# Summed squares, block layouts, in-place y and a gated opening in an eight-core decoder trunk

## The chip, the cores and the metric

The program runs on one Trainium2 chip, on all 8 cores. Each core computes half of one prompt (2048 of 4096 tokens, with a halo of 144 positions ahead of them that it computes again) and 64 of the 512 sample rows. No core talks to another. The metric is device time in microseconds (us) of the slowest core.

## The reference

Layer 0 is an attention and convolution layer, layer 1 a pooling layer. Around each mixer stand two half-step SwiGLU feed-forward blocks, so there are four in all:

```python
def rmsnorm(x, g):
    y = x * lax.rsqrt(jnp.mean(x * x, axis=-1, keepdims=True) + 1e-6)
    return y * g

# per layer
x = x + 0.5 * swiglu(rmsnorm(x, g[0]), gate, up, down)      # 1024 -> 2816 -> 1024
h = rmsnorm(x, g[1])
x = x + mixer(h)   # layer 0: windowed attention | short convolution, projected out
                   # layer 1: causal means over 2, 4, 8, 16 rows minus h, grouped linear
x = x + 0.5 * swiglu(rmsnorm(x, g[2]), gate2, up2, down2)
# at the end
y = rmsnorm(x, final_gain)
```

The outputs are y for prompt and sample tokens and the updated key, value, convolution and pooling states.

## The kernel before

Features lie on the partitions (8 tiles of 128, index `k` or `m`), tokens on the free axis. The 2256 tokens of a core are done in two groups one after the other: group 0 has 1168 tokens (144 halo, 1024 prompt), group 1 has 1088 (1024 prompt, 64 sample). A group is cut into three subs: 400, 384 and 384 columns in group 0, 384, 384 and 320 in group 1. Later stages of group 0 need fewer halo columns, and the first sub shrinks to 272 and then to 256. The sample tokens are the last 64 columns of group 1.

One Python function, `emit`, lists all operations in program order. `Sched.op` puts a semaphore wait wherever an operation reads or overwrites what another engine or a transfer touches. Each engine then runs its own operations strictly in that listed order. So the order of the listing sets what an engine is stuck behind; no planner moves anything.

- **Weights** go through a ring of 17024 bf16 columns. `pump` (L312) issues a transfer from the POOL queue as soon as space is free. Eight gate-and-up tiles fit; they are converted from f32 by the transfer.
- **Norms.** `Norm.sq` squares row `k` of x on ACT into a bf16 buffer, and `Norm.flush` lets PE multiply it by a column of 1/1024 (`onesD`), one matmul for each block of at most 128 tokens. These "ones matmuls" accumulate the mean of squares over the 8 rows. `Norm.stat` takes the root on ACT and the reciprocal on DVE, `Norm.rb` broadcasts it with f32 matmuls, and `Norm.hs` makes the scaled input h (`sb_hT`) with 8 DVE instructions.
- **ffn** has a staged first part (gate and up products, `evac` with Silu on ACT and a product on DVE) and then `rows_out` for the down product. A down row is 22 matmuls for one of the 8 rows `m` and one sub. In its middle `half` flushes the squares of an earlier row. DVE adds the row to x (`add`, L380 into `sb_xs`) and ACT squares the new x. The last 2 or 4 rows are done sub by sub, so that the norm of one sub is made beside the next (`ms`). Two PSUM banks (`yb`) take turns as the row's output. The last sub's norm is made at the start of the next stage (`tail_hooks`).
- **The mixer** makes k, q and v of all columns of a sub (`rope_unit`, `v_unit`), and in `chb_unit` the three products of the convolution branch. These units fill the PE between steps of the attention.
- **The pooling stage** (`pool_stage`) makes window sums as matmuls with scaled identities (`p_stage`), copies them to `pp` on ACT, and multiplies by the group weights (`z_stage`). The sums of the sample tokens are made by `sample_pool` on POOL (L1229, L1247), from an h that DVE writes, into `spp`. One DVE copy (L372) then puts all of `spp` into `pp` ahead of the third sub.
- **Ends.** At the start SP's queue loads constants and then x of group 0 (one sub in four pieces, two subs whole), and POOL's queue loads eight weight tiles. At the end `out_ops` writes y into one of two staging buffers (`ystg`, `sb_reg` in the profile) and stores it with one transfer for each sub. The third sub uses the first one's buffer again.

## Time and profile before

| | |
|---|---|
| runs of the kernel before | 2514.12, 2624.45 and 2623.94 us; median 2623.94 us |
| profiled execution | 2516.68 us |
| its span on the slowest core | 2515.1 us |
| spans of the eight cores | 2507.5 to 2515.1 us |
| PE (matmul) busy | 2409.5 us, 96% |
| DVE busy | 816.8 us, 32% |
| ACT busy | 587.7 us, 23% |
| POOL busy | 288.6 us, 11% |
| PE's share of the chain that ended last | 91% |

PE is busy for all but 105.6 us of the span. A row of the timeline gives the start in us, the busy time in us, the engine, the source line, the operation, what it writes and reads, the shape and the count; in brackets stands the idle time ahead of it and what ended it. Matmuls overlap, so the distance between two starts tells more of their price than the busy time does.

### The profile page before, as it was taken

The numbers are of one execution on the slowest core, as the hardware profiler recorded it, in microseconds if no ns is written. First come the engines' busy times: TensorE is split into PE (matmuls) and PEld (weight loads), VectorE is DVE, ScalarE is ACT, GpSimd is POOL, SyncE is SP. The second block draws the span as 40 slices with busy tenths as digits, with TensorE's granted clock in tenths as the row PEclk, the third lists the DMA queues.
The fourth block names the chain that finished last, engine by engine and source line by source line (L and its number), as shares of the span: only waits on it lengthen the run. The fifth ranks groups of instructions, "written<-read, shape, count | busy, mean of one in ns | idle before, by whom it ended". The sixth has DMA issues, their size and how long they took to land.

```text
span 2515.1 us, 45298 instructions; the slowest of 8 cores (2507.5 to 2515.1 us)
## 1 busy us (share of the span) xinstructions
PE 2409.5 (96%) x16668; PEld 1544.1 (61%) x16668; DVE 816.8 (32%) x1705; ACT 587.7 (23%) x1420; POOL 288.6 (11%) x512
## 2 busy tenths in 40 slices
PE   4999999999999999999999999999999999979996
PEld 2555655666666666666666665566666666646664
DVE  2221287522132214321432128752213221342213
ACT  3111145211111113212231114421111111221111
POOL 0001133000000010001000014300000000020000
PEclk9999999999999999999999999999999999989998
DMA  9544323344445442444574453245453544415432
GB/s 199 109 66 70 56 38 52 63 77 75 70 67 84 69 75 34 68 71 76 111 159 67 73 73 58 45 68 77 70 73 57 84 68 64 67 31 78 67 60 72
DMA packets 72407, 184.99 MB, mean 74 GB/s; under 512 B 9376, under 2 KB 24032, under 8 KB 72160
## 3 DMA queue, kind: packets, MB, share of 16 engines
q0 software_dynamic: 53424, 157.18, 41.5%
q1 hardware_dynamic: 18768, 24.90, 3.8%
q8 instruction: 140, 2.29, 0.4%
q14 instruction: 75, 0.61, 0.1%
HBM read 329.25 MB, written 11.99 MB: 136 GB/s over the span
## 4 chain that ended last, share of the span: by engine, by line
PE 91%; DVE 3%; DMA 3%; issue 1%; POOL 1%; ACT 1%; DVEq 0%; SPq 0%; ACTq 0%; POOLq 0%
PE ps_gupair L359 68%; PE ps_bk L359 22%; DMA sb_xs<-xin 2%; DVE sb_hT L380 1%; PE ps_bk L363 1%; DMA y_main<-sb_reg 0%; POOL sb_reg L1229 0%; ACT sb_sqr L407 0%; DVE sb_xs L380 0%; DVE sb_reg L380 0%; DVE sb_ovl L375 0%; DVE sb_xs L375 0%; POOL sb_reg L984 0%; DVE sb_rp L375 0%; POOL sb_reg L1247 0%
## 5 line engine op out<-in xcount | busy, mean ns | idle before, releaser
L359 PE MATMUL ps_gupair<-sb_hT,sb_wring 128*128 128x384 bf16 (+4 forms) x8696 | 1339.3, 316 | 4.4 <-DVE sb_xs L380 1.7
L359 PEld LDWEIGHTS ps_gupair<-sb_hT,sb_wring 128*128 128x128 bf16 x8696 | 849.9, 98 | 482.6 <-issue 11.9
L375 DVE TENSOR_TENSOR sb_ovl<-sb_rp,ps_gupair 128x384 bf16<-128x384 f32 (+4 forms) x536 | 282.8, 528 | 960.3 <-PE ps_gupair L359 942.8
L407 ACT ACTIVATE sb_rp<-ps_gupair 128x384 f32<-128x384 f32 (+4 forms) x528 | 247.4, 470 | 999.0 <-PE ps_gupair L359 997.3
L359 PE MATMUL ps_bk<-sb_ovl,sb_wring 128*128 128x384 bf16 (+4 forms) x2304 | 382.4, 316 | 1.4 <-DVE sb_xs L375 1.3
L359 PE MATMUL ps_gupair<-sb_ovl,sb_wring 128*128 128x384 bf16 (+4 forms) x2304 | 382.0, 315 | 0.0
L407 ACT ACTIVATE sb_sqr<-sb_xs 128x384 bf16<-128x384 f32 (+4 forms) x336 | 163.0, 501 | 647.8 <-DVE sb_xs L380 481.2
L359 PEld LDWEIGHTS ps_bk<-sb_ovl,sb_wring 128*128 128x128 bf16 x2304 | 216.6, 98 | 116.4 <-issue 3.4
L359 PEld LDWEIGHTS ps_gupair<-sb_ovl,sb_wring 128*128 128x128 bf16 x2304 | 216.3, 98 | 112.4
L327 POOL DMA_DIRECT2D sb_wring<-wgu x176 | 93.3, 532 | 1270.1 <-PE ps_gupair L359 1046.2
L380 DVE SCALAR_TENSOR_TENSOR sb_hT<-sb_xs,sb_cst,ps_bk 128x384 bf16<-128x384 f32 (+4 forms) x280 | 145.1, 582 | 9.0 <-PE ps_bk L359 9.0
L359 PE MATMUL ps_bk<-sb_hT,sb_wring 128*128 128x384 bf16 (+3 forms) x808 | 141.2, 320 | 5.0 <-DVE sb_reg L413 3.4
L380 DVE SCALAR_TENSOR_TENSOR sb_xs<-ps_gupair,sb_xs 128x384 f32<-128x384 f32 (+4 forms) x96 | 51.1, 532 | 268.7 <-PE ps_gupair L359 258.5
L327 POOL DMA_DIRECT2D sb_wring<-wd x128 | 67.5, 528 | 593.9 <-PE ps_gupair L359 466.6
L380 DVE SCALAR_TENSOR_TENSOR sb_xs<-ps_bk,sb_xs 128x384 f32<-128x384 f32 (+4 forms) x96 | 51.1, 532 | 227.3 <-PE ps_bk L359 221.6
L359 PEld LDWEIGHTS ps_bk<-sb_onesD,sb_sqr 128*128 128x128 bf16 (+2 forms) x984 | 70.4, 97 | 81.0 <-issue 53.4
L359 PE MATMUL ps_bk<-sb_onesD,sb_sqr 128*128 128x1 bf16 (+2 forms) x984 | 73.8, 166 | 47.9 <-ACT sb_sqr L407 46.7
L359 PEld LDWEIGHTS ps_bk<-sb_hT,sb_wring 128*128 128x128 bf16 x808 | 73.0, 98 | 56.6 <-issue 19.0
L984 POOL TENSOR_SCALAR sb_reg<-sb_reg,sb_st 128x256 bf16<-128x256 f32 x68 | 68.3, 1013 | 101.2 <-DVE sb_st L976 89.1
L407 ACT ACTIVATE sb_reg<-ps_gupair,sb_st 128x256 f32<-128x256 f32 x136 | 62.0, 465 | 4.5 <-DVE sb_st L390 4.5
L359 PE MATMUL ps_gupair<-sb_hT,sb_Dg 128*128 128x384 bf16 (+1 forms) x360 | 57.3, 315 | 1.2 <-ACT sb_reg L370 1.2
L359 PE MATMUL ps_bk<-sb_cst,sb_rr 128*128 128x128 f32 (+2 forms) x246 | 40.7, 301 | 10.9 <-DVE sb_rr L482 8.6
(111 smaller groups left out, 791.7 us busy)
## 6 DMA issues: line engine op xcount, KB each, us to landing
sb_wring<-wgu POOLq DMA_DIRECT2D x176, 512.0 KB, 5.7
sb_wring<-wd POOLq DMA_DIRECT2D x128, 352.0 KB, 5.0
sb_wring<-wmi POOLq DMA_DIRECT2D x46, 256.0 KB, 5.4
y_main<-sb_reg SPq DMA_DIRECT2D x4, 1536.0 KB, 16.4
sb_xs<-xin SPq DMA_DIRECT2D x3, 1536.0 KB, 40.6
sb_wring<-wmo POOLq DMA_DIRECT2D x16, 256.0 KB, 5.1
...
```

What stands on the lines that cost most here:

```text
L327: OP("pool", lambda e, d=dst, s=src: e.dma_start(out=d, in_=s), [], [[("wring", off * 2, (off + n) * 2)]], dma=f"w{t % NWK}")
L359: OP("pe", lambda e: e.matmul(out.ap, lhsT=lhsT.ap, rhs=rhs.ap, start=start, stop=stop), [lhsT, rhs], [out])
L363: OP("pe", lambda e: e.transpose(out.ap, in_.ap, idn.ap), [in_, idn], [out])
L375: OP(eng, lambda e: e.tensor_tensor(out=out.ap, in0=a.ap, in1=b.ap, op=op), [a, b], [out])
L380: OP("dve", lambda e: e.scalar_tensor_tensor(out=out.ap, in0=a.ap, scalar=sc, in1=b.ap, op0=op0, op1=op1), rd, [out])
L407: OP("act", lambda e: e.activation(out=out.ap, in_=in_.ap, func=func, **kw), rd, wr)
L984: OP("pool", lambda e, o_=o_, i_=i_, sc_=sc_: e.tensor_scalar(out=o_.ap, in0=i_.ap, scalar1=sc_.ap, scalar2=None, op0=ALU.mult), [i_, sc_] ...
```

## The change

It has these parts.

1. `Norm.sqa` stands in for `Norm.sq` in the four down products of both groups (`presum=True`). ACT squares row 0 into `rp(s.idx)` and every other row into `rp(3)`, both f32; DVE adds the two after each row, and after the last row writes the sum as bf16. PE then does one set of ones matmuls for each sub where it did eight. The other norms (after the mixers and of the loaded x) keep `sq`.
2. x and y lie in blocks in DRAM: each sub of x, and each stored piece of y, is contiguous for each partition. The host arranges them.
3. y of group 1 is written over x (`Y = X(s, k)`), and two rows at a time are stored as soon as they are made. Group 1's last down product goes in 4 + 4 rows where it was 6 + 2.
4. In the opening, x of subs 1 and 2 comes in two halves each; the weight transfers from the third tile on wait for the last piece of x of sub 0; mask, convolution state, cache copies, cosines and sines wait until the third tile of the first product is there.
5. Queries are made for columns from 128 on, gate and h products of the convolution from 126 on, where both were made from 0 on in group 0.
6. The sample tokens' pooling goes ahead of the scaled h of the third sub, and ACT copies its result row by row.

```diff
@@ Norm @@
+                def sqa(self, k, s):
+                    c = slice(0, s.n)
+                    if k == 0:
+                        act(rp(s.idx, c), X(s, k), AF.Square)
+                        return
+                    act(rp(3, c), X(s, k), AF.Square)
+                    if k < KC - 1:
+                        tt(rp(s.idx, c), rp(s.idx, c), rp(3, c), ALU.add)
+                        return
+                    sl = cnt["sq"] % NSQ
...
+                    tt(sqr(sl, c), rp(s.idx, c), rp(3, c), ALU.add)
+                    self.pend.append((None, s, sl))
@@ rows_out @@
-                    nxt.sq(m, ns)
+                    if presum:
+                        nxt.sqa(m, ns)
+                    else:
+                        nxt.sq(m, ns)
@@ pump @@
-                    OP("pool", lambda e, d=dst, s=src: e.dma_start(out=d, in_=s), [],
+                    OP("pool", lambda e, d=dst, s=src: e.dma_start(out=d, in_=s), gate.get(t, []),
@@ mixer @@
+                csubs = g.subs(max(g.mix - 2, 0))
-                    return [k_unit(s)] + [q_unit(j, s) for j in range(4)] + [v_unit(s)]
+                    return [k_unit(s)] + [q_unit(j, msubs[s.idx]) for j in range(4)] + [v_unit(s)]
-                fill = qkv(subs[1]) + qkv(subs[2]) + [chb_unit(i, s) for i in range(4) for s in subs]
+                fill = qkv(subs[1]) + qkv(subs[2]) + [chb_unit(i, s) for i in range(4) for s in csubs]
@@ pool_stage @@
                             copy(pp(k, slice(0, np_)), pbk(slice(0, np_)), eng="act")
+                            if np_ < n:
+                                copy(pp(k, slice(np_, n)), spp(k), eng="act")
-                    if g.i == 1 and si == 2:
-                        c0 = g.S[0] - s.c0
-                        copy(pp(slice(0, KC), slice(c0, c0 + 64)), spp(), eng="dve")
                                 norm.rb(norm.subs[2])
+                                if g.i == 1:
+                                    q.q += sample_pool(g, subs[2], norm)
+                                    q.pop()
                                 q.q += norm.hs(norm.subs[2])
                                 if g.i == 1:
                                     q.q += outs(subs[2])
-                                    q.q += sample_pool(g, subs[2], norm)
@@ out_ops @@
+                if g.i == 0:
+                    yt = ystg[s.idx % 2]
+                    Y = lambda k: yt(k, slice(0, s.n))
...
+                else:
+                    Y = lambda k: X(s, k)
+                    src = xs[s.slot].ap
+                    d = s.base
...
+                for k in range(KC):
+                    out.append(lambda k=k: stt(Y(k), X(s, k), cs(C_GAIN + 6 * 8 + k), norm.r(s), ALU.mult, ALU.mult))
+                    if g.i == 1 and k % 2 == 1:
+                        out.append(lambda k=k: store(k - 1, k + 1))
@@ opening @@
             load_x(GROUPS[0], 0, 4)
-            load_x(GROUPS[0], 1)
-            load_x(GROUPS[0], 2)
+            s0 = GROUPS[0].subs(0)[0]
+            load_x(GROUPS[0], 1, 2)
+            load_x(GROUPS[0], 2, 2)
...
+            gate[2] = [X(s0, KC - 1)]
             pump()
-            dma("pool", maskb.ap, maskd[:, :, :], [], [maskb()], "msk")
...
+            def later():
+                rd = [aT(2, slice(0, 400))]
+                dma("pool", maskb.ap, maskd[:, :, :], rd, [maskb()], "msk")
...
@@ last ffn @@
-                    ms=(4, 4) if g.i == 0 else (6, 2))
+                    ms=(4, 4))
```

How this stands on the engines is shown at three places.

The first is POOL's queue at the start of the program, `sb_wring` being the weight ring. Before:

```order
L1420 UNCONDITIONAL_BRANCH [waits barrier_Pool_Activation_PE_DVE_SP_gather]
L327 DMA sb_wring<-wgu 128x2048 x8
L410 DMA sb_maskb<-maskd 128x1536
L327 DMA sb_wring<-wgu 128x2048 [waits s_pe,d_w0]
L327 DMA sb_wring<-wgu 128x2048 [waits s_pe,d_w1]
```

And now:

```order
L1474 UNCONDITIONAL_BRANCH [waits barrier_Pool_Activation_PE_DVE_SP_gather]
L328 DMA sb_wring<-wgu 128x2048 x2
L328 DMA sb_wring<-wgu 128x2048 [waits d_x06]
L328 DMA sb_wring<-wgu 128x2048 x5
L328 DMA sb_wring<-wgu 128x2048 [waits s_pe,d_w0]
```

The third weight tile and the five behind it now wait for `d_x06`, the last piece of x of sub 0, and the mask has left this place.

The second is DVE's queue in group 1's pooling stage. `sb_reg` with 128x64 is the scaled h of the sample tokens, `sb_h1c` the pooling state, `sb_hT` h of the norms. Before, from the second sub to the start of the third:

```order
L380 SCALAR_TENSOR_TENSOR sb_reg<-sb_xs,sb_cst,ps_bk 128x64 x3
L380 SCALAR_TENSOR_TENSOR sb_hT<-sb_xs,sb_cst,ps_bk 128x384 x4
L380 SCALAR_TENSOR_TENSOR sb_xs<-ps_bk,sb_cst,sb_xs 128x384
L380 SCALAR_TENSOR_TENSOR sb_xs<-ps_gupair,sb_cst,sb_xs 128x384
L380 SCALAR_TENSOR_TENSOR sb_hT<-sb_xs,sb_cst,ps_bk 128x384 x4
L372 COPY sb_reg<-sb_ovl 128x8x64
L380 SCALAR_TENSOR_TENSOR sb_xs<-ps_bk,sb_cst,sb_xs 128x320
```

And now, from the last rows of the down product ahead of the stage into its first sub:

```order
L381 SCALAR_TENSOR_TENSOR sb_xs<-ps_gupair,sb_xs 128x320
L376 TENSOR_TENSOR sb_sqr<-sb_rp 128x320
L381 SCALAR_TENSOR_TENSOR sb_hT<-sb_xs,sb_cst,ps_bk 128x384 x8
L504 RECIPROCAL sb_rr<-sb_rt 128x2
L504 RECIPROCAL sb_rr<-sb_rt 64x1
L381 SCALAR_TENSOR_TENSOR sb_xs<-ps_bk,sb_cst,sb_xs 128x384
L381 SCALAR_TENSOR_TENSOR sb_xs<-ps_gupair,sb_cst,sb_xs 128x384
L381 SCALAR_TENSOR_TENSOR sb_reg<-sb_xs,sb_cst,ps_bk 128x64 x8
L381 SCALAR_TENSOR_TENSOR sb_xs<-ps_bk,sb_cst,sb_xs 128x384
```

The eight sample rows moved from the second sub to the first, the copy of 128x8x64 is gone from DVE's queue, and the sum of squares stands between the last addition to x and the eight rows of h.

The third is DVE's queue at the end of the program. Before, `sb_reg` is the staging buffer of y:

```order
L380 SCALAR_TENSOR_TENSOR sb_reg<-sb_xs,sb_cst,ps_bk 128x384 x3
L380 SCALAR_TENSOR_TENSOR sb_xs<-ps_gupair,sb_xs 128x320
L380 SCALAR_TENSOR_TENSOR sb_reg<-sb_xs,sb_cst,ps_bk 128x384 x8
L482 RECIPROCAL sb_rr<-sb_rt 128x2
L482 RECIPROCAL sb_rr<-sb_rt 64x1
L380 SCALAR_TENSOR_TENSOR sb_reg<-sb_xs,sb_cst,ps_bk 128x320 x8
```

And now:

```order
L381 SCALAR_TENSOR_TENSOR sb_xs<-sb_xs,sb_cst,ps_bk 128x384 x3
L381 SCALAR_TENSOR_TENSOR sb_xs<-ps_gupair,sb_xs 128x320
L376 TENSOR_TENSOR sb_sqr<-sb_rp 128x320
L381 SCALAR_TENSOR_TENSOR sb_xs<-sb_xs,sb_cst,ps_bk 128x384
L504 RECIPROCAL sb_rr<-sb_rt 128x2
L504 RECIPROCAL sb_rr<-sb_rt 64x1
L381 SCALAR_TENSOR_TENSOR sb_xs<-sb_xs,sb_cst,ps_bk 128x320 x8
```

Seven of the eight y rows of the second sub now stand ahead of the last addition to x, and one stands behind it, where eight stood before.

## Rows read from the trace of the kernel before

**Rows 1.** The page: its first line and its part 1.

```profile
span 2515.1 us, 45298 instructions; the slowest of 8 cores (2507.5 to 2515.1 us)
PE 2409.5 (96%) x16668; PEld 1544.1 (61%) x16668; DVE 816.8 (32%) x1705; ACT 587.7 (23%) x1420; POOL 288.6 (11%) x512
```

**Rows 2.** The timeline of the opening: start us, busy us, engine, instruction, count [idle ahead].

```profile
31.31 0.96 ACT L407 ACTIVATE sb_sqr<-sb_xs 128x400 bf16<-128x400 f32 x2 [6.20 <-DMA sb_xs<-xin]
...
36.51 7.88 PE L359 MATMUL ps_gupair<-sb_hT,sb_wring 128*128 128x400 bf16 x24 [0.88 <-DVE sb_hT L380]
```

**Rows 3.** The same timeline from 43 us on.

```profile
44.41 1.76 ACT L407 ACTIVATE sb_sqr<-sb_xs 128x384 bf16<-128x384 f32 x4 [11.33 <-DMA sb_xs<-xin]
```

**Rows 4.** Transfers by queue from 8 to 17 us: packets, MB, share of 16 engines.

```profile
q0 software_dynamic: 305, 1.12, 75.7%
q1 hardware_dynamic: 305, 0.46, 24.4%
```

**Rows 5.** Transfers by queue from 45 to 52 us.

```profile
q1 hardware_dynamic: 1153, 2.01, 122.5%
```

**Rows 6.** The timeline of group 1's last down product.

```profile
2455.79 0.31 PE L359 MATMUL ps_bk<-sb_onesD,sb_sqr 128*128 128x1 bf16 x3
2456.03 1.96 PE L359 MATMUL ps_gupair<-sb_ovl,sb_wring 128*128 128x384 bf16 x11
2457.83 1.66 PE L359 MATMUL ps_bk<-sb_ovl,sb_wring 128*128 128x320 bf16 x11
...
2459.33 0.22 PE L359 MATMUL ps_bk<-sb_onesD,sb_sqr 128*128 128x1 bf16 x3
2459.40 1.65 PE L359 MATMUL ps_bk<-sb_ovl,sb_wring 128*128 128x320 bf16 x11
```

**Rows 7.** The timeline where group 0 goes from its second to its third block.

```profile
724.19 0.56 DVE L380 SCALAR_TENSOR_TENSOR sb_xs<-ps_gupair,sb_xs 128x384 f32<-128x384 f32 x1 [2.07 <-PE ps_gupair L359]
724.66 4.28 DVE L380 SCALAR_TENSOR_TENSOR sb_hT<-sb_xs,sb_cst,ps_bk 128x384 bf16<-128x384 f32 x8
724.89 0.52 ACT L407 ACTIVATE sb_sqr<-sb_xs 128x384 bf16<-128x384 f32 x1 [3.33 <-DVE sb_xs L380]
...
728.86 0.17 DVE L482 RECIPROCAL sb_rr<-sb_rt 128x3 f32<-128x3 f32 x1
...
729.18 0.91 PE L359 MATMUL ps_bk<-sb_cst,sb_rr 128*128 128x128 f32 x6 [2.17 <-DVE sb_rr L482]
```

**Rows 8.** The timeline of group 0's first mixer part.

```profile
319.96 6.93 PE L359 MATMUL ps_gupair<-sb_hT,sb_wring 128*128 128x400 bf16 x40
...
329.25 0.57 DVE L375 TENSOR_TENSOR sb_ovl<-sb_rp 128x400 bf16<-128x400 f32 x1
```

**Rows 9.** The timeline of a down product of group 0 with 272 columns.

```profile
704.81 1.44 PE L359 MATMUL ps_gupair<-sb_ovl,sb_wring 128*128 128x272 bf16 x11
706.08 0.22 PE L359 MATMUL ps_bk<-sb_onesD,sb_sqr 128*128 128x1 bf16 x3
```

**Rows 10.** The timeline of group 1's pooling stage.

```profile
2206.52 0.32 POOL L1229 TENSOR_TENSOR sb_reg<-sb_reg 128x64 f32<-128x64 f32 x1 [24.57 <-DVE sb_reg L380]
...
2228.16 0.29 DVE L372 COPY sb_reg<-sb_ovl 128x512 bf16<-128x512 bf16 x1 [10.77 <-POOL sb_ovl L1229]
2228.61 0.69 PE L359 MATMUL ps_bk<-sb_reg,sb_wring 128*128 128x320 bf16 x2 [12.27 <-DVE sb_reg L372]
```

**Rows 11.** The stretch behind it: us, busy times, granted clock (PEclk), DMA share, GB/s.

```profile
2228.60:2233.60 5.00, 4.99 (x23) 3.21 (x24) 1.08 (x2) 0.64 (x2) 0.00 (x0) 0.50 0.00 0
```

**Rows 12.** The timeline of the end.

```profile
2492.19 1.66 PE L359 MATMUL ps_gupair<-sb_ovl,sb_wring 128*128 128x320 bf16 x11
...
2494.37 4.28 DVE L380 SCALAR_TENSOR_TENSOR sb_reg<-sb_xs,sb_cst,ps_bk 128x384 f32<-128x384 f32 x8
...
2505.09 3.75 DVE L380 SCALAR_TENSOR_TENSOR sb_reg<-sb_xs,sb_cst,ps_bk 128x320 f32<-128x320 f32 x8 [6.31 <-DMA y_main<-sb_reg]
2509.50 0.68 SPq L410 DMA_DIRECT2D y_samp<-sb_reg  x1
```

86 lines of the change are left out of this document (59 added, 27 removed).

## The prediction

> **What bounds the kernel now.** I read the page first [rows 1]. PE is busy for 2409.5 of 2515.1 us, so only two things can pay: matmul work that goes away, and the 105.6 us in which PE stands. The timeline of PE, read for its brackets, then shows that the standing is not spread out. The opening holds a third of it: the first product of the first block begins at 36.51 us [rows 2]. Group 1's pooling stage has one stop of 12.27 us [rows 10]. After the last down matmuls 21 us pass until the end [rows 12]. In between PE runs almost without a gap, and DVE, ACT and POOL wait for it. An edit that only relieves those three is worth nothing there.
>
> The sum is made against the profiled execution's 2516.68 us, which is 1.6 us more than its span. The runs shown are 2514.12, 2623.94 and 2624.45 us for one and the same kernel, so the median of 2623.94 stands 4.3% above the execution that I can read; my sum is for the level of 2516.68.
>
> **The opening.** The fourth and last piece of x of sub 0 is there at 31.31 us, and 5.2 us later the first product starts [rows 2]; that chain of squares, root, broadcast and scaling is the same after the change. What makes x late is sharing: from 8 to 17 us the queue of POOL (q0, weights) and that of SP (q1, x) move 305 packets each, but 1.12 MB against 0.46 MB [rows 4]. A weight packet takes 0.757 x 16 x 9 / 305 = 357 ns of an engine, an x packet of 1.5 KB 115 ns. After the change only two weight tiles (1.05 MB) stand against the constants and x of sub 0 (1.9 MB). By these prices the weights take 6.4 us on 16 engines. x takes 9.1 us at the rate of rows 4, or 6.6 us at that of q1 alone, 2.01 MB in 7 us [rows 5]. With some 2 us before anything moves, x is complete at 15 to 18 us. I take 17, so 14 us sooner. The third weight tile is issued then and is wanted after two units. The first unit and a half, 24 matmuls, took 7.88 us [rows 2], so that is about 10 us after the 5.2 us chain, and a tile that takes turns with x, 8 packets per engine at (357 + some 400) ns, needs 6 us. So the gate should cost nothing; uncovered, it costs up to 6 us. x of sub 1 came at 44.41 us [rows 3], about when the first unit was over, and held the second by about 1 us; it now comes some 20 us sooner. Together **-15**, ends -9 and -19. Larger packets in the block layout only help here, and I book nothing for them elsewhere: later loads of x and group 0's stores lie beside products.
>
> **The ones matmuls.** Each down product did eight sets, now one. Blocks of at most 128 tokens add up to 10 + 9 + 9 + 8 in group 0 and 4 x 9 in group 1, so 72, and 7 x 72 = 504 matmuls go. Their price is not the 0.22 or 0.31 us of busy time but the hole that they make. Three full blocks start at 2459.33 and the product goes on at 2459.40, 0.07 us; the set with a partial block runs from 2455.79 to 2456.03, 0.24 us [rows 6]. Seven of the eight down products have one such sub and two full ones: 7 rows x (0.24 + 2 x 0.07) = 2.7 us; group 0's last has 7 x 3 x 0.07 = 1.5 us. Sum 7 x 2.7 + 1.5 = **-20**. Ends: every matmul at 0.07 / 3, -12, and at 0.24 / 3, -40. I take the rows as they fall.
>
> The Trainium skill (TensorE: Matmul & The Clock Gate, Back-to-back issue gap) gives about 81 ns for each pair of weight load and short matmul in a stream. By that figure, as an estimate, 504 pairs would be 41 us and the sum 21 us better; the full blocks in the trace are far below it, the set with a partial block is at it.
>
> **What the DVE sum costs.** 168 additions of 128x384 f32, 0.57 us each by the nearest row, one with both inputs in SBUF [rows 8]. A down row takes PE 2 x 1.80 = 3.6 us [rows 6]. DVE's work in it is the addition to x, 0.56, then the wait until ACT's square ends, 0.66 (724.89 + 0.52 against 724.75), then 0.57: 1.8 us. With five rows of h (4.28 / 8 = 0.54 each, rows 7) it is 4.5 us, in one row of each sub; two output banks give a row of slack, so PE does not feel it. It does at the end of a down product. There DVE began eight rows of h right after the last addition to x, and the reciprocal for the last sub stands behind them: 728.86 us, and PE stood 2.17 us for it [rows 7]. Now DVE first waits for the square and then sums: 0.66 + 0.57 with the handing over, 1.3 us more. This boundary binds already; the others have slack of unknown size. Eight boundaries x 1.3 = 10 at most, plus some delay of the first bank in the mixer; none at least. **+6**, ends 0 and +12.
>
> **Halo columns.** In group 0's first sub 4 x 2 x 8 matmuls for queries shrink from 400 to 272 columns: 6.93 / 40 = 173 ns [rows 8] against 1.27 / 11 = 115 ns [rows 9], so 64 x 0.058 = 3.7 us. The same count for gate and h goes to 274 columns, 3.6 us. In the first stretch DVE is nearly full with rope and the rows of h, so the queries may give only half. **-6**, ends -3 and -7.
>
> **Group 1's pooling.** POOL worked on the sample sums from 2206.52 to 2228.16 us; DVE's copy waited 10.77 us for it, and with it PE 12.27 us [rows 10]. Behind that PE ran 5.0 us at a granted clock of 0.50, the lower of its levels [rows 11], which cost 2.5 us. Now the eight sample rows are written about one sub (17 us) sooner, and POOL's 21.6 us should end about 2211, when the third sub's first product, which came right before the stop at 2216, is not yet due. The copies go row by row on ACT, some 0.2 us each, and can hold PE there about 1 us. 12.3 + 2.5 - 1 = **-14**, ends -8 (POOL ends late by 5 us) and -15.
>
> **The end.** The last product ends at 2493.85 us, the span at 2515.1: 21.3 us [rows 12]. In it DVE wrote eight y rows of sub 1 (4.28 us), and waited 6.31 us for the staging buffer before the last eight; then came the two stores. The chain after the change: addition 0.6, square 0.6, sum 0.6, ones 0.3, root and reciprocal 0.7, broadcast 1.6 at the lower clock, eight y rows 3.9, issue of the last pair 0.6, landing 3: 12 us. The landing is bounded by 2 us and by the 5.2 us that the last stores took (2515.1 less 2509.5 with the issue begun). **-9**, ends -5 and -12. That group 1 now does four rows sub by sub moves no matmul.
>
> **Sum.** -15 - 20 + 6 - 6 - 14 - 9 = -58, so 2516.7 - 58 = 2459 us. All ends at once would be -25 to -93; since they are independent, about 19 us on either side is what I allow: 2440 to 2478.
>
> **Rivals.**
>
> A. *Dearer ones matmuls.* If each costs what one in the partial set does, 0.08 us, then 504 give 40 and the time is 2439. For it: the row of 0.24. Against it: the two rows in three that show 0.07 for three. The Trainium skill's 81 ns on the page named above is this case. 0.11.
>
> B. *The gains are half taken back.* The third weight tile is late because x now comes in 6 KB packets that get the larger part of each turn (opening -9), each boundary pays its 1.3 us and more (+12), DVE holds the queries (-3), POOL's work stretches over its new place (-10), the stores queue on SP (-6), ones -20: -36, 2481 us. For it: PE's wait of 2.17 us is on just that chain. Against it: each part would have to fall to its worse half together. 0.18.
>
> C. *DVE becomes the pace of the down products, slower than before.* Place: DVE's add, wait, sum in each of 192 down rows. At 4.0 us a row where PE needs 3.6, the loss is 192 x 0.4 = 77 us, 2536 us. It decides from 3.9 us a row on (58 us over 192 rows is 0.3 us), which asks 2.6 us for an addition for which the nearest row has 0.57. 0.03.
>
> D. *The change does not do what it says*: the gate opens too late to matter because x of sub 0 is bound by its own packets, and the rest holds: opening -2, time 2472. For it: no row shows a packet of 3.2 KB, which x of sub 0 now has. Against it: the equal counts, which say that fewer weight packets mean fewer turns lost. 0.02.
>
> **How the numbers follow.** Forecast 0.66, A 0.11, B 0.18, C 0.03, D 0.02. I call the time faster or slower when it is more than 2% away, 50 us here (below 2466), which is about what a measurement of this kernel tells from no change. Of the forecast's 0.66 some four fifths lie beyond 50 us, 0.54, with A 0.65. Slower is C, 0.03. The rest is within 2%, 0.32. The low end is A's side of the forecast, 2438. B's 2481 lies just past the forecast's own upper end. The upper end of the whole range must hold one more thing: the time on record is a median of few runs, and two of three runs of the kernel before were 4.4% above the third. The same step on 2459 gives 2567, and I give it 0.3 whatever the case, so the range goes to 2570; the forecast's own range is 2440 to 2478.
>
> **What would show it.** Opening: first square of x's last piece near 17 us, first product near 22, no wait for a weight tile after it. Ones matmuls: half the count, and down rows of 3.6 us with no hole. Boundaries: the wait for the reciprocal at group 0's second to third block grows from 2.17 to about 3.5 us. Pooling: no wait of PE above 2 us and no stretch at a clock of 0.50. End: about 12 us from the last product. I am wrong if PE waits for weights in the opening, if PE waits for additions in mid-product, or if the PE time of the down products falls by less than 12 us.

## The result and the profile after

The changed kernel's ratio to the kernel before is **0.9864, 95% interval [0.9836, 0.9893]**: 34 us less, inside the 2% that was called no change. The profiled execution took 2481.2 us, 35.5 us under the one before. The prediction said 2459 us, and 2440 to 2478 us around it; the undisturbed executions took 2479.4, 2481.0 and 2481.2 us. (The medians on record, 2669.48 us for the changed kernel and 2569.57 us for the one before, contain executions in which one die or both ran at a lower clock; such executions are left out of every ratio and range below.)

The page's first lines, and two groups of its part 5 (busy time, mean ns | idle time ahead and what ended it), against [rows 1]:

```profile
span 2479.6 us, 44427 instructions; the slowest of 8 cores (2471.1 to 2479.6 us)
...
PE 2390.5 (96%) x16164; PEld 1528.0 (62%) x16164; DVE 902.2 (36%) x1872; ACT 589.3 (24%) x1428; POOL 288.1 (12%) x512
...
L376 DVE TENSOR_TENSOR sb_rp<-sb_rp 128x384 f32<-128x384 f32 (+4 forms) x144 | 76.7, 533 | 108.7 <-ACT sb_rp L408 107.8
...
L360 PE MATMUL ps_bk<-sb_onesD,sb_sqr 128*128 128x1 bf16 (+2 forms) x480 | 34.1, 166 | 36.8 <-ACT sb_sqr L408 31.0
```

PE has 504 matmuls fewer, as counted. But its busy time fell by 19 us only, and 89 us of standing are left of 105.6. Of DVE's sums, all but the last of each sub stand in the second row: each waits some 0.75 us for ACT's square, 107.8 us together.

Where the time went shows when the span is cut at the first matmul of each stage. The table has the length of each stage in us, as the median of eight cores, from the timelines of PE; the last three columns are kernels 1, 4 and 14 of the next section. "gate k" and "down k" are the two parts of ffn k; stages that no kernel changed by 1 us are left out. (The expectations quoted below say group one and two for groups 0 and 1, and block 2 for ffn 2.)

| stage | before | changed | no sum | two sets | two sets, rows of h behind |
|---|---|---|---|---|---|
| start to the first product | 36.5 | 23.0 | 23.1 | 23.1 | 23.1 |
| group 0: gate 0 | 185.6 | 183.5 | 183.6 | 183.4 | 183.7 |
| down 0 | 93.0 | 90.3 | 93.0 | 90.5 | 90.5 |
| mixer, first part | 17.2 | 17.0 | 15.8 | 15.7 | 15.7 |
| attention | 116.6 | 114.8 | 114.8 | 115.0 | 115.0 |
| down 1, down 2, each | 82.1 | 79.4 | 82.1 | 79.8 | 79.8 |
| gate 2 | 158.4 | 161.5 | 158.4 | 158.5 | 156.2 |
| pooling | 44.1 | 46.7 | 43.8 | 45.4 | 45.4 |
| group 1: gate 0 | 169.8 | 173.2 | 170.3 | 170.6 | 171.4 |
| down 0 | 86.1 | 84.6 | 86.1 | 83.8 | 83.8 |
| mixer, first part | 15.9 | 17.0 | 15.8 | 15.8 | 15.8 |
| attention | 122.3 | 122.5 | 123.3 | 122.5 | 122.4 |
| mixer's output product | 37.5 | 38.7 | 38.9 | 38.8 | 38.8 |
| down 1 | 85.2 | 83.3 | 85.2 | 82.7 | 82.8 |
| gate 2 | 164.5 | 167.7 | 164.5 | 164.5 | 163.6 |
| down 2 | 85.2 | 83.2 | 85.2 | 82.7 | 82.7 |
| pooling | 59.3 | 49.9 | 48.8 | 48.0 | 48.1 |
| down 3 | 85.3 | 82.8 | 85.3 | 82.9 | 82.9 |
| last product to the end | 17.8 | 13.1 | 11.3 | 12.0 | 11.9 |

The last row differs much between cores of the kernel before: 17.2 to 21.3 us, where the changed kernel has 12.5 to 13.3. The 21.3 us from which the prediction started is the slowest core.

The opening, the downs, group 1's pooling and the end got shorter. The stages *behind* the downs got longer, by 14.7 us together: gate 2 in both groups, group 0's pooling, and group 1's gate 0, mixer and output product.

**Opening.** The timeline of PE, against [rows 2]; then the transfers of 8 to 17 us by queue, against [rows 4]:

```profile
18.66 0.76 PE L360 MATMUL ps_bk<-sb_onesD,sb_sqr 128*128 128x1 bf16 x8 [0.60 <-ACT sb_sqr L408]
20.13 2.16 PE L360 MATMUL ps_bk<-sb_cst,sb_rr 128*128 128x128 f32 x8 [0.71 <-DVE sb_rr L504]
23.31 8.43 PE L360 MATMUL ps_gupair<-sb_hT,sb_wring 128*128 128x400 bf16 x24 [1.02 <-DVE sb_hT L381]
```
```profile
q1 hardware_dynamic: 433, 1.31, 51.7%
q0 software_dynamic: 216, 0.75, 50.5%
```

The queue of x (q1) moves 1.31 MB in these 9 us where it moved 0.46, and the first product comes at 23.31 us.

**A boundary.** The timeline of group 0 from down 1 to gate 2, all engines, against [rows 7]; then busy times and the granted clock (last number but two) behind it:

```profile
703.34 0.56 DVE L376 TENSOR_TENSOR sb_sqr<-sb_rp 128x384 bf16<-128x384 f32 x1 [0.84 <-ACT sb_rp L408]
703.81 4.28 DVE L381 SCALAR_TENSOR_TENSOR sb_hT<-sb_xs,sb_cst,ps_bk 128x384 bf16<-128x384 f32 x8
...
704.04 0.21 PE L360 MATMUL ps_bk<-sb_onesD,sb_sqr 128*128 128x1 bf16 x3 [0.37 <-DVE sb_sqr L376]
...
708.01 0.17 DVE L504 RECIPROCAL sb_rr<-sb_rt 128x3 f32<-128x3 f32 x1
...
708.33 0.91 PE L360 MATMUL ps_bk<-sb_cst,sb_rr 128*128 128x128 f32 x6 [3.07 <-DVE sb_rr L504]
```
```profile
707.40:710.00 2.60, 1.67 (x13) 1.53 (x14) 1.76 (x6) 0.00 (x0) 0.00 (x0) 0.93 0.00 0
710.00:713.40 3.40, 3.40 (x14) 1.73 (x13) 3.40 (x8) 0.21 (x1) 0.00 (x0) 0.55 0.00 0
713.40:716.00 2.60, 2.60 (x18) 1.56 (x16) 1.13 (x3) 0.45 (x2) 0.00 (x0) 1.00 0.00 0
```

DVE waits 0.84 us for the last square, adds, and only then begins the eight rows of h (4.28 us) behind which the reciprocal stands. PE stops for 0.37 us at the ones matmuls and for 3.07 instead of 2.17 us at the broadcast. Then it runs 3.4 us at a granted clock near 0.5 (the lower of its levels, 1.2 GHz), which costs another 1.7 us. 0.37 + 0.90 + 1.7 = 3.0 us: the 3.1 us of the table.

**Down rows**, the timeline of group 1's last, against [rows 6]; and **the mixer's first part**, against [rows 8]:

```profile
2442.37 0.22 PE L360 MATMUL ps_bk<-sb_onesD,sb_sqr 128*128 128x1 bf16 x3
2442.45 1.95 PE L360 MATMUL ps_gupair<-sb_ovl,sb_wring 128*128 128x384 bf16 x11
...
2446.68 3.74 PE L360 MATMUL ps_bk<-sb_ovl,sb_wring 128*128 128x384 bf16 x22
```
```profile
302.93 0.91 PE L360 MATMUL ps_bk<-sb_cst,sb_rr 128*128 128x128 f32 x6 [1.73 <-DVE sb_rr L504]
303.67 4.80 PE L360 MATMUL ps_gupair<-sb_hT,sb_wring 128*128 128x272 bf16 x40
310.20 2.01 PE L360 MATMUL ps_gupair<-sb_hT,sb_wring 128*128 128x272 bf16 x16 [1.73 <-DVE sb_rp L376]
```

These down rows run without a hole (2442.45 to 2446.68 are 22 matmuls and a broadcast). In the mixer 40 query matmuls take 4.80 us for 6.93, and PE then waits for DVE.

In group 0's last down product there is a hole, on every core, that the kernel before and kernel 1 (below) don't have, while kernel 4 has it too. PE's timeline:

```profile
1190.42 2.56 PE L360 MATMUL ps_gupair<-sb_ovl,sb_wring 128*128 128x256 bf16 x22
1194.25 2.56 PE L360 MATMUL ps_bk<-sb_ovl,sb_wring 128*128 128x256 bf16 x22 [1.26 <-DVE sb_xs L381]
```

PE waits in mid-product until DVE has added an earlier row to x and the bank is free, which the prediction had named as a sign of being wrong.

**Pooling of group 1 and the end**, against [rows 10] and [rows 12]:

```profile
2204.10 0.21 PE L360 MATMUL ps_bk<-sb_onesD,sb_sqr 128*128 128x1 bf16 x3 [2.43 <-ACT sb_sqr L408]
...
2463.81 2.88 PE L360 MATMUL ps_gupair<-sb_ovl,sb_wring 128*128 128x320 bf16 x20
...
2469.61 0.39 PE L360 MATMUL ps_bk<-sb_onesD,sb_sqr 128*128 128x1 bf16 x3 [2.91 <-DVE sb_sqr L376]
...
2472.39 3.75 DVE L381 SCALAR_TENSOR_TENSOR sb_xs<-sb_xs,sb_cst,ps_bk 128x320 f32<-128x320 f32 x8 [1.76 <-PE ps_bk L360]
...
2477.07 0.47 SPq L411 DMA_DIRECT2D y_samp<-sb_xs  x1
```

The stop of 12.27 us is gone; the longest left in that stage is 2.43 us. Right behind it PE works at the lower clock again:

```profile
2204.70:2208.10 3.40, 3.40 (x18) 2.28 (x18) 1.08 (x2) 0.85 (x5) 0.00 (x0) 0.50 0.00 0
```

The last product ends at 2466.7 us, and 12.9 us later all is stored, where it was 21.3.

### The profile page after: what moved, and what is told of

Same layout as the page of the kernel before. It is cut to its first block, busy times and chain, and to the rows that moved or that the text cites. A ratio compares the mean times of both kernels' runs of the same rounds, so it can differ in the third digit from the quotient of the medians.

```text
span 2479.6 us, 44427 instructions; the slowest of 8 cores (2471.1 to 2479.6 us)
## 1 busy us (share of the span) xinstructions
PE 2390.5 (96%) x16164; PEld 1528.0 (62%) x16164; DVE 902.2 (36%) x1872; ACT 589.3 (24%) x1428; POOL 288.1 (12%) x512
## 4 chain that ended last, share of the span: by engine, by line
PE 89%; DVE 6%; issue 2%; DMA 2%; ACT 1%; POOL 0%; DVEq 0%; SPq 0%; ACTq 0%; POOLq 0%
PE ps_gupair L360 68%; PE ps_bk L360 21%; DVE sb_hT L381 3%; DMA y_main<-sb_reg 1%; DVE sb_xs L381 1%; DMA sb_xs<-xin 1%; PE ps_bk L364 1%; ACT sb_sqr L408 0%; DVE sb_ovl L376 0%; DVE sb_st L986 0%; ACT sb_rp L408 0%; DVE sb_rp L376 0%; DVE sb_rp L381 0%; DVE sb_reg L381 0%; POOL sb_reg L1010 0%
## 5 line engine op out<-in xcount | busy, mean ns | idle before, releaser
L360 PE MATMUL ps_bk<-sb_ovl,sb_wring 128*128 128x384 bf16 (+4 forms) x2304 | 373.2, 316 | 2.6 <-DVE sb_xs L376 1.4
L360 PE MATMUL ps_gupair<-sb_ovl,sb_wring 128*128 128x384 bf16 (+4 forms) x2304 | 375.0, 316 | 0.0
L360 PEld LDWEIGHTS ps_bk<-sb_ovl,sb_wring 128*128 128x128 bf16 x2304 | 223.5, 98 | 126.6 <-issue 4.4
L360 PEld LDWEIGHTS ps_gupair<-sb_ovl,sb_wring 128*128 128x128 bf16 x2304 | 222.2, 98 | 119.6 <-issue 0.2
L408 ACT ACTIVATE sb_rp<-sb_xs 128x384 f32<-128x384 f32 (+4 forms) x192 | 96.4, 502 | 525.1 <-DVE sb_xs L381 525.0
L376 DVE TENSOR_TENSOR sb_rp<-sb_rp 128x384 f32<-128x384 f32 (+4 forms) x144 | 76.7, 533 | 108.7 <-ACT sb_rp L408 107.8
L408 ACT ACTIVATE sb_sqr<-sb_xs 128x384 bf16<-128x384 f32 (+4 forms) x144 | 66.8, 500 | 84.9 <-DVE sb_xs L376 47.1
L360 PE MATMUL ps_bk<-sb_onesD,sb_sqr 128*128 128x1 bf16 (+2 forms) x480 | 34.1, 166 | 36.8 <-ACT sb_sqr L408 31.0
L360 PEld LDWEIGHTS ps_bk<-sb_onesD,sb_sqr 128*128 128x128 bf16 (+2 forms) x480 | 30.7, 97 | 51.8 <-issue 42.4
```

The source lines that it names most:

```text
L360: OP("pe", lambda e: e.matmul(out.ap, lhsT=lhsT.ap, rhs=rhs.ap, start=start, stop=stop), [lhsT, rhs], [out])
L376: OP(eng, lambda e: e.tensor_tensor(out=out.ap, in0=a.ap, in1=b.ap, op=op), [a, b], [out])
L408: OP("act", lambda e: e.activation(out=out.ap, in_=in_.ap, func=func, **kw), rd, wr)
```

## The experiments

My theory: the sum on DVE is worth about 16 us of ones matmuls and gives the same back at the boundaries, since the last addition stands in the chain that PE waits for there.

**1. No sum** (changed kernel, every square to PE again).

```diff
-   rows_out(..., hs or nxt.hs, beside, presum=True)
+   rows_out(..., hs or nxt.hs, beside)
```

> The changed kernel with one part undone: the squares of all eight down rows go to TensorE again, eight sets of ones products a sub-tile. My theory: the sum on DVE takes some 16 us off the down products (stage by stage: 2.7, 2.65, 2.65, 0.2, 1.5, 1.9, 1.95 and about 2.8 us) and gives some 14.7 us back behind them (gate of block 2 3.1, pooling of group one 2.6, first gate of group two 3.5, its mixer 1.1, its output products 1.2, its gate of block 2 3.2 us), because the last square is added on DVE before the ones products may start, and TensorE's longer stop there is followed by a stretch at a granted clock of 0.50. Then this kernel's down products are longer by 16 us, the stages behind them shorter by 13 to 15 us, and the time is 2483 us (2479 to 2487), a ratio to the kernel before of 0.987 against 0.9864 of the whole change. The rival, by the prediction's own sizes (sum worth 20, boundaries costing 6, the stretches of lower clock due to another part of the change): the gates behind the down products stay as long as in the changed kernel and the time is 2495 us, a ratio of 0.992.

2480.4 us, ratio 0.9858 [0.9842, 0.9873]. As the theory has it. The eight downs are 16.1 us longer; by the table the other stages are 14.3 us shorter and the end 1.7. (The 1.2 us of the mixer's output product in group 1 stay without the sum, so they are not its doing.) Medians of stages leave out what only some cores have: by the means of the eight cores the others are 11.8 us shorter and the end 1.7, so that the mean core is 2.6 us slower than in the changed kernel. The slowest core, which sets the time, is as fast. The sum, as it was written, is worth nothing there.

**2. Halo columns back.**

```diff
-   [q_unit(j, msubs[s.idx]) for j in range(4)]
+   [q_unit(j, s) for j in range(4)]
-   [chb_unit(i, s) for i in range(4) for s in csubs]
+   [chb_unit(i, s) for i in range(4) for s in subs]
```

> The changed kernel with one part undone: the mixer's queries and the conv gate products are computed for the halo columns again. My theory: the first part of the mixer waits for DVE there, so its queries' fewer columns gave nothing, and of the conv gate products only some 2 us were gained in the attention stage of group one; the time is 2483 us (2481 to 2485). The rival, by the prediction: 6 us were gained by fewer columns and lost elsewhere; then the time is 2487 us, the mixer and the attention stage of group one together 6 us longer.

2482.0 to 2484.7 us, ratio 0.9870 [0.9851, 0.9889]. The stages are 18.35 us (mixer) and 117.0 us (attention): 1.4 + 2.2 = 3.6 us, between theory and rival. I had put the queries at nothing; they give 1.4 us, though PE waits for DVE there.

**3. The sum alone**, on the kernel before.

```diff
+   def sqa(self, k, s):
...
+   nxt.sqa(m, ns)
...
+   rows_out(..., hs or nxt.hs, beside, presum=True)
```

> The kernel before with nothing but the summed squares of the down rows on DVE. My theory: the down products are shorter by some 13 to 16 us in all, and the stages behind them longer by 12 to 15 us (a longer wait of TensorE for the last block's ones products and reciprocal, and a lower granted clock behind it), so the time is 2513 us (2509 to 2517), a ratio of 0.999. The rival, by the prediction's sizes of 20 and 6: 2501 us, a ratio of 0.9945, with the boundaries each under 1 us longer.

Ratio 1.0012 [1.0002, 1.0022]: the sum by itself makes the kernel a little slower, 3 us, and seven of its eight executions (2515.3 to 2523.1 us) lie past the theory's upper end of 2517; the rival's 2501 is out. The downs fall as in the changed kernel (82.1 to 79.4 us), gate 2 grows to 161.5 and 168.0 us.

**4. Two sets.** DVE sums rows 0 to 6; row 7's square goes to PE as a second set.

```diff
+   if k == KC - 1:
+       self.sq(k, s)
+       return
    act(rp(3, c), X(s, k), AF.Square)
-   if k < KC - 1:
+   if k < KC - 2:
        tt(rp(s.idx, c), rp(s.idx, c), rp(3, c), ALU.add)
        return
...
-   not k and i == 0, k in (None, KC - 1) and i == len(bl) - 1)
+   not k and i == 0, k == KC - 1 and i == len(bl) - 1)
```

> The changed kernel, but DVE sums only the squares of rows 0 to 6 of a down product; the square of row 7 goes from ACT to TensorE as a second set of ones products, so that no addition on DVE stands between the last square and the ones products. My theory: of the 14.7 us given back at the boundaries about half goes (the DVE addition of some 0.5 us and its place behind other DVE rows at eight places, and 1.7 us for each of some 3 to 5 stretches of lower clock that are not triggered then), against 1 to 3 us for the second sets of ones products (24 sets of 0.07 to 0.24 us): 2475 us (2470 to 2480), a ratio of 0.984. The rival, that the stop at a boundary is set by the rows of h that DVE and ACT have to do behind the reciprocal and not by the sum: the same stops as in the changed kernel, and 2483 us.

2464.7 us, ratio **0.9797 [0.9783, 0.9811]**: 16 us faster than the changed kernel, more than I forecast. The same boundary in its timeline, all engines:

```profile
702.44 4.28 DVE L381 SCALAR_TENSOR_TENSOR sb_hT<-sb_xs,sb_cst,ps_bk 128x384 bf16<-128x384 f32 x8
...
703.54 0.29 PE L360 MATMUL ps_bk<-sb_onesD,sb_sqr 128*128 128x1 bf16 x6
...
706.64 0.17 DVE L507 RECIPROCAL sb_rr<-sb_rt 128x3 f32<-128x3 f32 x1
...
707.06 0.95 PE L360 MATMUL ps_bk<-sb_cst,sb_rr 128*128 128x128 f32 x3 [2.28 <-DVE sb_rr L507]
```

No wait at the ones matmuls, and a stop of 2.28 us, as before the change. Three of group 0's downs keep all but 0.3 us of their gain, and three of group 1's gain 0.5 to 0.8 us more. Of the 14.7 us in the six longer stages 11.3 came back; 4.2 more came in group 0's mixer, group 1's pooling and the end.

**5, 6. Rows of h behind the reciprocal**, with the full sum and with two sets. The rows of the sub that is done stand in a queue `q`; the last five are kept for the next stage.

```diff
+   if keep:
+       q.pop(max(len(q.q) - keep, 0))
+       left.extend(q.q)
+       q.q = []
...
    norm.stat(norm.subs[2])
+   q.q += left
+   left.clear()
```

> The changed kernel, the sum on DVE left as it is, with one thing moved: at the end of a down product (not of the last ffn) DVE does three of the eight rows of h of the second sub-tile ahead of the last sub-tile's reciprocal, and the other five behind it. My theory: TensorE's stop at the boundary is DVE's queue (wait for the last square, sum, eight rows of h of 4.28 us, reciprocal), so with five rows fewer ahead of it the stop of 3.07 us falls to about 0.5 us and the stretch at a granted clock of 0.50 behind it goes too: gate of block 2 shorter by 3 to 5 us in each group, pooling by 1 to 3, mixer by about 1; 2467 us (2462 to 2474). The rival: the five rows are missed by the next sub-tile's products and the wait only moves there, 2481 us.

> Both at once: DVE sums the squares of rows 0 to 6 only, row 7's square goes to TensorE as a set of its own, and five rows of h go behind the reciprocal. My theory: the stop of 2.3 us which stayed with the two sets goes as well, since DVE has then neither the sum nor the five rows ahead of the reciprocal: 2456 us (2451 to 2461). The rival, that the rows of h are missed later: 2465 us as with the two sets alone, the gain of the boundary found again as waits for sb_hT or for additions in the first products of the second sub-tile.

Ratios 0.9816 [0.9801, 0.983] and 0.9812 [0.9796, 0.9829], 2468.6 to 2472.5 us both. The first is my theory, at the upper part of its range: without touching the sum, 10 us come back. Gate 2 is 4.2 and 4.3 us shorter, as it said, and group 1's pooling 1.7; but both mixers are 0.8 us longer and not 1 shorter. The second fell: it is no faster than two sets alone (the intervals overlap, and every execution took longer than those of kernel 4). Its stages say why. Gate 2 is 156.2 and 163.6 us (2.3 and 0.9 us gained), but each mixer's first part is 2.2 us longer and group 0's pooling 1.2 us. PE's timeline of that mixer, in kernel 6 and then in kernel 4:

```profile
302.22 3.20 PE L361 MATMUL ps_gupair<-sb_hT,sb_wring 128*128 128x272 bf16 x24
307.65 2.01 PE L361 MATMUL ps_gupair<-sb_hT,sb_wring 128*128 128x272 bf16 x16 [2.23 <-DVE sb_rp L377]
311.41 2.01 PE L361 MATMUL ps_gupair<-sb_hT,sb_wring 128*128 128x272 bf16 x16 [1.75 <-DVE sb_rp L377]
```
```profile
303.18 4.81 PE L360 MATMUL ps_gupair<-sb_hT,sb_wring 128*128 128x272 bf16 x40
309.75 2.01 PE L360 MATMUL ps_gupair<-sb_hT,sb_wring 128*128 128x272 bf16 x16 [1.75 <-DVE sb_rp L376]
```

In the mixer DVE is full with the rotations behind the reciprocal, so five rows of h put among them are paid at once. Ahead of a gate they are not.

**7. A known delay** ahead of the reciprocal, on kernel 4.

```diff
    norm.flush()
+   for _ in range(3):
+       tt(dum(), dum(), dum(), ALU.mult)   # 128x224 f32
    norm.stat(norm.subs[2])
```

> The kernel with two sets, with nothing but a known delay added: three DVE products of 128x224 f32, some 0.35 us each, about 1.05 us in all, stand ahead of the last sub-tile's reciprocal at the start of each gate stage behind a mixer, a down product or a pooling (six places). My theory, that a longer stop itself brings down the granted clock behind it: gate of block 2 grows in both groups by the 1.05 us and by another 1.7 us for a stretch at a granted clock of 0.50, from 158.5 to 161.3 us and from 164.5 to 167.3, as in the changed kernel; the whole 2474 us (2470 to 2480), as some of the other four places have slack. The rival, that the lower clock in the changed kernel has another cause than the length of the stop: the gates grow by 1.05 us at most, 159.6 and 165.6 us, the whole 2469 us.

2470.4 to 2473.0 us, ratio 0.9821 [0.9804, 0.9837]. The three products took 1.38 us, not 1.05. Gate 2 of group 0 takes 161.46, 159.80, 161.47 and 159.79 us on cores 0 to 3, and gate 2 of group 1 165.78 on all four: 1.3 us for the delay everywhere, and 1.67 us more on two cores, in one place. PE's stop on cores 0 and 1, and the granted clock right behind it:

```profile
708.91 1.33 PE L361 MATMUL ps_bk<-sb_cst,sb_rr 128*128 128x128 f32 x6 [3.57 <-DVE sb_rr L508]
...
709.03 0.91 PE L361 MATMUL ps_bk<-sb_cst,sb_rr 128*128 128x128 f32 x6 [3.57 <-DVE sb_rr L508]
```
```profile
708.00:711.00 3.00, 2.09 (x11) 1.75 (x12) 1.53 (x6) 0.00 (x0) 0.00 (x0) 0.71 0.00 0
...
708.00:711.00 3.00, 1.97 (x16) 1.74 (x17) 1.96 (x6) 0.00 (x0) 0.00 (x0) 1.00 0.00 0
```

The same stop of 3.57 us, to the hundredth, was followed by a lower clock on one core and not on the other. So the length of this one stop does not decide it. At gate 2 of group 0, behind a stop of 2.17 us, it came on one of eight cores in the kernel before, on three in kernel 1 and on five in kernel 11; behind 2.28 us on two of eight in kernel 4; behind 3.57 us on two of four here. On all eight it came only where a stop of 0.37 us stood ahead of one of 3.07, in the changed kernel and in kernel 3. Neither theory nor rival is right as written, and why the changed kernel has it on every core is not shown. The Trainium skill (TensorE: Matmul & The Clock Gate, Terms) puts the penalty at the time spent throttled times one minus the ratio of the rates; 3.4 us at half rate is 1.7 us by it, and the 1.67 us between cores agrees.

**8. Pooling and end back** to the order of before (one DVE copy ahead of the third sub; group 1's y staged and stored whole), on kernel 4.

```diff
    q.q += norm.hs(norm.subs[2])
+   if g.i == 1:
+       q.q += outs(subs[2])
+       q.q += sample_pool(g, subs[2], norm)
...
+   copy(pp(slice(0, KC), slice(c0, c0 + 64)), spp(), eng="dve")
...
-   if g.i == 0:
+   if True:
        yt = ystg[s.idx % 2]
...
-   ms=(4, 4))
+   ms=(4, 4) if g.i == 0 else (6, 2))
```

> The kernel with two sets, with two parts of the change undone that lie in different stages: in group two's pooling the sample sums stand again behind the rows of h and the outputs, with DVE's one copy; and group two's y goes through the staging buffers again, stored whole, with six rows tile by tile and two sub by sub in its last down product. By what the changed trace showed against the one before: pooling of group two 48.0 to 58.5 us (+10.5), and from the last product to the end 13 to 21 us (+8), the whole 2483 us (2480 to 2486). The rival, by the prediction's sizes, +14 and +9 with something else having taken the difference in the changed kernel: pooling 62 us and 2488 us.

2479.3 to 2482.7 us, ratio 0.9856 [0.9837, 0.9876], as expected in sum. Pooling is 59.1 us, 11.1 more, and the stop is back:

```profile
2201.29 0.29 DVE L373 COPY sb_reg<-sb_ovl 128x512 bf16<-128x512 bf16 x1 [10.33 <-POOL sb_ovl L1258]
2201.73 0.69 PE L360 MATMUL ps_bk<-sb_reg,sb_wring 128*128 128x320 bf16 x2 [11.84 <-DVE sb_reg L373]
```

From the last product to the end it takes 16.8 us, on the slowest core and on the median one, where kernel 4 takes 12.0 and the kernel before 21.3 (slowest) or 17.8 (median). The transfers of y in that stretch (KB each, median us from issue to landing), on the slowest core of the kernel before and then here:

```profile
y_main<-sb_reg SPq DMA_DIRECT2D x2, 1536.0 KB, 10.6
```
```profile
y_main<-sb_reg SPq DMA_DIRECT2D x2, 1536.0 KB, 6.4
```

With y in blocks the same 1.5 MB land in 6.4 us, and DVE's wait of 6.31 us for the staging buffer [rows 12] does not occur. Over the eight cores these stores took 5.8 to 11.7 us in the kernel before and 5.5 to 6.8 us here, and only three cores of the kernel before waited for the buffer. So the rows in place are worth 4.8 us, on all cores alike (16.5 to 16.9 us here, 11.7 to 12.2 in kernel 4). The layout of y, taken first, is worth 4.5 us on the slowest core and 1.0 on the median one: it takes away the late stores of a few cores. (Rows in place without the layout were not run; they have no staging buffer to wait for either, so the split holds in this order only. Kernel 8 also has two sets where the kernel before has eight; what that does to the end was not told apart.)

**9. No gate** in the opening, on kernel 4.

```diff
-   gate[2] = [X(s0, KC - 1)]
```

> The kernel with two sets, with the gate of the opening undone: the third weight tile and those behind it are issued at once and don't wait for the last piece of x of sub-tile 0; the block layout of x, the split loads and the late loads of mask, states and caches stay. By the prediction's reckoning the weight packets then take their turns against x again: x of sub-tile 0 is complete some 6 us later (23 to 26 us in place of about 18), the first product starts at 29 us in place of 23, and the whole is 2470 us (2467 to 2474). The rival, that the layout and the loads taken out of the way did it and the gate nothing: first product within 1 us of 23, 2465 us.

2470.7 to 2472.8 us, ratio 0.9822 [0.9807, 0.9838]: the theory's time, and a first product between theory and rival. PE's timeline:

```profile
22.42 0.76 PE L360 MATMUL ps_bk<-sb_onesD,sb_sqr 128*128 128x1 bf16 x8 [3.55 <-ACT sb_sqr L408]
...
27.07 3.20 PE L360 MATMUL ps_gupair<-sb_hT,sb_wring 128*128 128x400 bf16 x6 [1.02 <-DVE sb_hT L381]
```

By the medians of the cores the first product comes 4.4 us later. So the gate is a third of the opening's 13.5 us, and 9 us belong to the layout of x and the loads put off, which the prediction had not told apart.

**10, 14. Rows of h behind the reciprocal at gate 2 only**, on kernel 4 (`keep=(5 if f == 1 else 0)`). It was timed twice; the first time gave no interval (2461.4 and 2464.9 us).

> The kernel with two sets, with five rows of h put behind the reciprocal only where a gate stage of the same width follows (ffn 1 to ffn 2, both groups), not ahead of the mixer and of the pooling. My theory, from the run with rows put behind at all places, in which those two gates got 2.3 and 0.85 us shorter, each mixer 2.2 and the pooling 1.2 us longer: here only the first part remains, so 2461.5 us (2459 to 2464), a ratio of 0.9785. The rival, that the moved rows also cost later in the gate (DVE's work is the same): 2465 us.

> The kernel with two sets and the five rows of h behind the reciprocal at the two gates only, timed once more with more rounds. From the stages of its profile against the kernel with two sets alone (gate of block 2 156.19 for 158.51 and 163.64 for 164.49 us, else alike): 2461.5 us (2459 to 2464), a ratio of 0.9785; the rival 2465 us, 0.9797.

2460.7 to 2463.2 us, ratio **0.9780 [0.9764, 0.9795]**, the lowest of all and as forecast to a microsecond. Its interval overlaps that of kernel 4; by stages the gain is 2.3 and 0.9 us in the two gates, and the median core is 3.2 us faster, though group 1's gate 0 is 0.8 us longer. The boundary, all engines:

```profile
702.54 1.65 DVE L382 SCALAR_TENSOR_TENSOR sb_hT<-sb_xs,sb_cst,ps_bk 128x384 bf16<-128x384 f32 x3
...
703.64 0.29 PE L361 MATMUL ps_bk<-sb_onesD,sb_sqr 128*128 128x1 bf16 x6
...
704.38 0.18 DVE L508 RECIPROCAL sb_rr<-sb_rt 128x3 f32<-128x3 f32 x1 [0.19 <-ACT sb_rt L409]
704.47 2.16 DVE L382 SCALAR_TENSOR_TENSOR sb_hT<-sb_xs,sb_cst,ps_bk 128x384 bf16<-128x384 f32 x4
704.81 0.91 PE L361 MATMUL ps_bk<-sb_cst,sb_rr 128*128 128x128 f32 x6
```

The reciprocal no longer stands behind h, and PE does not stop at all. This shows what the 2.28 us of kernel 4 were made of, and, as the same rows stand in the same place there [rows 7], the 2.17 us before the change.

**11. Two sets alone**, on the kernel before.

> The kernel before with nothing but the squares of rows 0 to 6 of the down products summed on DVE and row 7's square as a second set. My theory: down products shorter by 2.4 us each (0 in group one's last), no boundary longer, so seven gains of about 2.3 us: 2500 us (2497 to 2504), a ratio of 0.9935, where the full sum alone gave 1.0012. The rival, that DVE's sum costs elsewhere too once the rest of the change is away: 2513 us.

2503.9 to 2509.7 us, with one of 2519.7; ratio 0.9965 [0.9949, 0.9981]. Between theory and rival: the downs gain as in kernel 4, but group 1's gate 0 is 173.3 us (before 169.8), and gate 2 of group 0 has more of the lower clock (160.0 for 158.4). About 9 us of the 16.8 that the downs give arrive.

**12, 13. Group 0's last y block in place**, on kernel 14 and on the changed kernel. In the changed kernel DVE waited at group 1's gate 0 for the store of the first block to leave the staging buffer, on four of eight cores and up to 6.02 us (the timeline of DVE; none in the kernel before):

```profile
1238.60 2.19 DVE L381 SCALAR_TENSOR_TENSOR sb_reg<-sb_xs,sb_cst,ps_bk 128x384 f32<-128x384 f32 x4 [6.02 <-DMA y_main<-sb_reg]
```
```diff
-   if g.i == 0:
+   if g.i == 0 and s.idx < 2:
        yt = ystg[s.idx % 2]
```

> The changed kernel with one thing altered: group one's last y block (sub-tile 2) is computed in place in x, whose slot group two does not use, so that DVE does not wait for sub-tile 0's store to leave the staging buffer. My theory: the 3.5 us by which group two's first gate stage grew (169.75 to 173.2, and 171.0 to 175.7 from core to core) are that wait of DVE (2.5 to 6.0 us on four cores, none in the kernel before) and what stands behind it; then this stage is 170.2 us (169.8 to 171.0) on every core and the whole 2477.5 us (2476 to 2480). The rival, that the stage is longer because the x of group two and the weights come late, or by the lower clock: 172 us or more on some cores, with waits for sb_sqr and sb_hT, and 2481 us.

> The kernel with two sets and the five rows of h behind the reciprocal at the two gates, and group one's last y block in place besides. My theory: group two's first gate stage 171.4 to 170 us and no core with more than 171, so the slowest core gains more than the median one: 2459 us (2457 to 2462), a ratio of 0.9775. The rival, that the slowest core is set by stretches of lower clock elsewhere: 2462 us.

Kernel 13: 2478.4 and 2478.7 us, without an interval; the slowest core's span falls from 2479.6 to 2476.5 us. The wait for the store is gone, but the stage is 173.5 us at the median, as before the edit; only the worst core went from 175.7 to 174.5. My theory was wrong for all but the worst cores. What PE waits for there now, in its timeline:

```profile
1231.07 0.21 PE L360 MATMUL ps_bk<-sb_onesD,sb_sqr 128*128 128x1 bf16 x3 [1.45 <-DVE sb_sqr L376]
...
1242.57 0.91 PE L360 MATMUL ps_bk<-sb_cst,sb_rr 128*128 128x128 f32 x6 [0.89 <-DVE sb_rr L504]
...
1247.14 0.67 PE L360 MATMUL ps_bk<-sb_onesD,sb_sqr 128*128 128x1 bf16 x6 [1.97 <-ACT sb_sqr L408]
```

The first is the sum again, and without it (kernels 1 and 4) the stage is 170.3 and 170.6 us. The others are the norms of the new x; the kernel before stands there too, up to 0.9 us each time. Kernel 12: 2460.8 to 2464.2 us, ratio 0.9784 [0.9768, 0.98], no better than 14, as its rival has it.

## Why the prediction was wrong

The forecast was 58 us, and the profiled executions differ by 35.5. No single term makes up the difference; the sum of squares makes up half of it, and there the prediction had a step wrong.

- **Opening, -15.** Right: 13.5 us to the first product and 2.2 in gate 0, 15.7 together. The forecast of 17 us for the last piece of x and 22 for the first product was met within 1.5 us, and PE waited for no weight tile. The gate, which the prediction had priced, gave 4.4 us of it (kernel 9); the other 9 came with the layout and the late loads, which it had not priced apart, so that the sum fits is in part luck.
- **Ones matmuls, -20.** The price from [rows 6] held in group 0, where 2.7 us a down product were forecast and 2.65 to 2.7 came. It failed for group 0's last down product (0.2 for 1.5 us, with the hole of 1.26 us shown above), and in three of group 1's (1.5 to 2.0 for 2.7, where PE also waits some 0.4 us for a reciprocal in the middle). With 2.6 in group 1's last one, 16 us. Rival A fell with it. So did the estimate of 41 us by the Trainium skill's 81 ns a pair (TensorE: Matmul & The Clock Gate, Back-to-back issue gap), which is the page's figure for matmuls of 128 columns; these have one.
- **What the DVE sum costs, +6.** This is the step that failed. Its own upper end was 12; it came out at 14.7 by the table and 14.3 by kernel 1 (11.8 by the means of the cores). The mechanism was named and the 1.3 us for DVE's delay was right (0.37 + 0.90 us at gate 2). Two things were missing. The delay was priced as time of PE standing, without the lower clock behind it, 1.67 us a time: in stretches of lower clock PE worked some 7 us more in the changed kernel than in kernel 1, which costs 3.5 us (means of eight cores, from the clock and PE's busy time of each stage). And "the others have slack of unknown size" was taken as slack: the mixer, the pooling and group 1's gate 0 had none. So the sum as a whole, for which the prediction had -20 + 6 = -14, gave nothing on the slowest core and 2.6 us on the mean one. Kernel 4, which takes one addition of eight out of this chain, got 16 us for it.
- **Halo columns, -6.** 3.6 us by kernel 2. The 4.80 us for 40 queries was foreseen, and part of it went into the wait for DVE at 310.20 us.
- **Pooling, -14.** 10.5 us (kernel 1 against before) or 11.1 (kernel 8). The stop of 12.27 us went, but PE waits 2.43 us for ACT in that stage now, and the 2.5 us booked for the lower clock did not come: "no stretch at a clock of 0.50" was wrong on all eight cores. PE's idle time in the stage fell by 10.8 us (16.9 to 6.1, mean of the cores, kernel 1 against before), and what it lost by working at the lower clock stayed the same (2.4 and 2.6 us).
- **End, -9.** 8.4 us from slowest to slowest core, but half of it came with the layout of y (kernel 8), for which nothing had been booked. On the median core the end gave 4.7 us, since that core had 17.8 and not 21.3 us to start from.

The sum of what was measured is -15.7 - 16 + 14.5 - 3.6 - 10.5 - 8.4 = -39.7, from medians of stages and the end of the slowest cores, which do not belong together. By the means of eight cores the span fell by 36.1 us: -15.8 for the opening, -16.1 for the downs, +11.8 behind them, -3.6 for the halo, -10.7 for the pooling and -5.3 for the end make -39.7 too, and 3.6 us were lost where no term had looked, 2.1 of them in group 1's attention and output product (kernel 1 against before). The slowest core, which sets the time, fell by 35.5: it reached the last down product 24.6 us sooner (its gate 0 of group 1 took 175.7 us where the median is 173.2, and it had more of the lower clock), which with 2.6 and 8.4 us behind it makes the 35.5.

Rival B, given 0.18, had the time (2481 us) and four of six terms within 2.5 us: boundaries +12, queries -3, pooling -10, stores -6. Its time is in part luck: its opening was 6.7 us too small, and its ones matmuls were 4 us too large. It was held unlikely because "each part would have to fall to its worse half together". What these four parts have in common is that each ends at a place where PE waits for DVE or ACT, and such a place can keep some of a gain; that this is why they fell together is argued and not tested.
